# The first modulation blocks of a two-block transformer kernel with the weight tile as the moving operand of TensorE, and another order at the stage's end

## The chip, the cores and the metric

The kernel runs on one core of one Trainium2 chip. The metric is the device time in microseconds (us), the median of several executions; lower is better. Engines are named as in the profile: PE is TensorE's matmul, PEld its weight load, DVE VectorE, ACT ScalarE, POOL GpSimd, SP the engine that issues the DMAs. Sizes in MB are 10^6 bytes.

## The reference

Two transformer blocks on one sequence of 256 tokens, width 2048, in fp32. Only the head of the first block matters here:

```python
c_act = jax.nn.silu(c)                              # [1, 2048]
mod = c_act @ w_ada[l] + b_ada[l]                   # w_ada: [2048, 12288]
sh1, sc1, gt1, sh2, sc2, gt2 = jnp.split(mod, 6, axis=-1)
h = modulate(rmsnorm(x, g_norm_mix[l]), sh1, sc1)   # rmsnorm(x) * (1 + sc1) + sh1
proj = h @ w_in[l]                                  # w_in: [2048, 3072]
```

After it come a gated linear recurrence and a pooling mixer, an output projection, a gated feed-forward layer and a second block with attention and a state-space part. The vector times matrix product `c_act @ w_ada` reads 100 MB of weights for one row of result, and `w_in` cannot start before the first third of it (shift and scale) is there.

## The kernel before

The program is written by hand, one instruction stream for each engine, with semaphores between them. The columns of `w_ada` are cut into 12 blocks of 1024 columns, and each block into 16 row chunks of 128: a **slot** is one chunk of one block, 128x1024 fp32, 0.524 MB. The **first stage** works off blocks 0 to 3 (`MOD_FIRST`, shift and scale, in the order `MOD_ORDER`): 64 slots, through a ring of 8 buffers (`mod_raw` and `mod_more`). The other blocks are spread over later phases.

The order of everything is fixed in the code. SP issues the slots in order; the DMA of slot s waits until slot s-8 has been used (`load_first`, L477). In the same queue stand the small vectors (L544), x (L546) and the four 1.05 MB tiles of `w_in`'s first block (L498), at the places of the table `w_in_at`. A table `mod_on_pe` gives each slot to one of two engines: in blocks 0 and 1 the odd chunks are PE's, in blocks 2 and 3 the chunks 1, 4, 7, 10 and 13; that is 26 slots for PE and 38 for DVE.

- DVE's share (L1972, L1976): `mod_acc = slot * c_silu[:, k] + mod_acc`, an elementwise sum over chunks that leaves 128 partial sums in each column.
- PE's share (`first_product`, L1245): eight matmuls with a 128x128 piece of the slot as the stationary operand and the one column `c_silu[:, k:k+1]` moving. The result is one PSUM column for each 128 outputs.
- `first_sums` (L1253) at a block's end: eight more such matmuls add DVE's partial sums over the partitions onto the same PSUM columns. `first_result` (DVE, L1982) adds the bias and signals `mod_ready`.

PE's stream in the stage also holds the transposes of the small vectors (`turn_vectors`, L1224, behind chunk 11 of block 0, which wait until all the small loads have landed), four blocks of transposes of x (`turn_block`, L1161) and, behind chunk 15 of block 2 and chunks 5 and 11 of block 3, halves 0, 1 and 2 of `w_in`'s first block (`first_w_in`, L1108 to L1110). A **half** is two row chunks by 512 columns, 24 matmuls with 256 moving columns; it needs ACT's `w_hi` (L613) and DVE's `w_lo` (L1719), the split of the raw tile, and two chunks of the normed and modulated input, `a_hi` and `a_lo` (L700, L1815), which DVE scales in `scaled` (L1994). Halves 0 to 3 need blocks 0 and 1 of the modulation only, halves 4 to 7 need all four.

After the last sums SP may overwrite old buffers with `gates_w` and `pool_w` (it waits for a POOL memset, L461, that waits for `mod_mm`), and only then issues the next tiles of `w_in` (L498) and slots 66 and up (L486). Then the phase `w_in` runs: for each of its 48 halves ACT and DVE split, DVE works off 1.25 slots (`mod_beside`, L1950), and PE does 24 matmuls.

```python
for m in range(MOD_M):        # PE, one slot, before: L1244
    mm = pe.matmul(first_column(i, m), first_slot(s)[:, m * P:(m + 1) * P], c_silu[:, k:k + 1],
                   start=(k == 1 and m == 0), stop=False, skip_group_check=True)
```

## Time and profile before

| | |
|---|---|
| median of 3 runs | 2711.17 us (2710.86 to 2712.18) |
| the profiled execution | 2713.19 us, its span 2711.5 us |
| mean granted clock of TensorE | 0.982 of full speed |
| PE busy | 2637.1 us (97%) |
| PEld busy | 2250.8 us (83%) |
| DVE busy | 1655.9 us (61%) |
| ACT busy | 1246.0 us (46%) |
| the 16 DMA engines | 548.50 MB, mean 202 GB/s over the span |

The shares of the whole span say little of a stage of some 130 us at its start. So the views of that stretch count: the windows (busy time of each engine, granted clock and DMA rate by stretch), the chain of waits (what released what) and the timeline.

### The profile page before, as it was taken

To read this page: it belongs to the slowest core of one execution; us is meant where nothing else is said; L and a number is where in the kernel's file an instruction comes from. 1 tells how busy PE (TensorE), PEld (TensorE's weight loads), DVE (VectorE), ACT (ScalarE), POOL (GpSimd) and SP (SyncE) were. 2 spreads that over 40 slices of the span, in tenths; PEclk is the share of its full clock that TensorE was granted. 3 is DMA by queue.
4 is the path that set the end of the run, shared out by engine and by line. 5 is a ranking of instruction groups with operands and counts; after the bars stand their busy time and mean duration, and the time that the engine had idled before them with its cause. 6 is when DMAs were issued, how large, how long until landed. Compare 5 with 4: busy or idle time off the path is not lost.

```text
span 2711.5 us, 34305 instructions
## 1 busy us (share of the span) xinstructions
PE 2637.1 (97%) x13318; PEld 2250.8 (83%) x13318; DVE 1655.9 (61%) x1954; ACT 1246.0 (46%) x1591; POOL 5.6 (0%) x24
## 2 busy tenths in 40 slices
PE   8999989999999999989999999999999999999998
PEld 8989767888888888878899988888888888888877
DVE  3598887674545444454866677555666666644445
ACT  2146335444444434443566555444555555544453
POOL 0000000000000000000000000000000000000000
PEclk9899999999999999988999999999999999999999
DMA  8897897885555555544543443555555555555554
GB/s 310 307 380 267 314 356 243 282 272 186 186 186 189 183 188 182 181 151 135 176 140 110 156 140 123 173 188 192 185 184 184 185 184 185 186 194 187 182 202 140
DMA packets 350003, 548.50 MB, mean 202 GB/s; under 512 B 18481, under 2 KB 200769, under 8 KB 349249
## 3 DMA queue, kind: packets, MB, share of 16 engines
q1 hardware_dynamic: 349888, 546.90, 59.9%
q8 instruction: 82, 1.34, 0.2%
q14 instruction: 33, 0.26, 0.0%
HBM read 544.74 MB, written 2.10 MB: 202 GB/s over the span
## 4 chain that ended last, share of the span: by engine, by line
PE 85%; DVE 6%; DMA 4%; ACT 3%; issue 2%; SPq 1%; ACTq 0%; DVEq 0%
PE pair L1133 23%; PE pair L1135 23%; PE pair L1134 23%; DMA mod_raw<-in_w_ada 3%; PE pair L1245 2%; PE pair L1108 2%; PE pair L1109 2%; PE pair L1110 2%; DVE mod_acc L1950 2%; DVE w_lo L1719 1%; PE misc L1161 1%; PE pair L1646 1%; ACT w_hi L613 1%; PE misc L1581 1%; PE misc L1699 1%
## 5 line engine op out<-in xcount | busy, mean ns | idle before, releaser
L1719 DVE TENSOR_TENSOR w_lo<-raw,w_hi 128x1024 fp32r<-128x1024 f32 x848 | 1017.4, 1204 | 877.4 <-ACT w_hi L613 876.2
L613 ACT ACTIVATE w_hi<-raw 128x1024 fp32r<-128x1024 f32 x848 | 882.0, 1043 | 1120.1 <-PE pair L1135 1027.0
L1133 PE MATMUL pair<-w_hi,a_hi 128*128 128x512 f32 x1856 | 733.8, 395 | 9.0 <-DVE w_lo L1719 3.8
L1135 PE MATMUL pair<-w_hi,a_lo 128*128 128x512 f32 x1856 | 725.7, 391 | 0.0
L1134 PE MATMUL pair<-w_lo,a_hi 128*128 128x512 f32 x1856 | 725.2, 391 | 0.0
L1133 PEld LDWEIGHTS pair<-w_hi,a_hi 128*128 128x128 f32 x1856 | 350.4, 189 | 82.8 <-issue 6.7
L1135 PEld LDWEIGHTS pair<-w_hi,a_lo 128*128 128x128 f32 x1856 | 350.0, 189 | 74.0
L1134 PEld LDWEIGHTS pair<-w_lo,a_hi 128*128 128x128 f32 x1856 | 350.4, 189 | 71.9 <-issue 1.0
L1133 PE MATMUL pair<-w_hi,hid_hi 128*128 128x512 f32 x704 | 274.7, 390 | 0.0
L1135 PE MATMUL pair<-w_hi,hid_lo 128*128 128x512 f32 x704 | 274.0, 389 | 0.0
L1134 PE MATMUL pair<-w_lo,hid_hi 128*128 128x512 f32 x704 | 273.9, 389 | 0.0
L1108 PE MATMUL pair<-a_hi,w_hi 128*128 128x256 f32 x768 | 228.2, 297 | 14.4 <-issue 8.6
L1109 PE MATMUL pair<-a_lo,w_hi 128*128 128x256 f32 x768 | 221.8, 289 | 0.0
L1110 PE MATMUL pair<-a_hi,w_lo 128*128 128x256 f32 x768 | 221.6, 289 | 0.0
L1108 PEld LDWEIGHTS pair<-a_hi,w_hi 128*128 128x128 f32 x768 | 152.2, 198 | 19.4 <-issue 9.1
L1950 DVE SCALAR_TENSOR_TENSOR mod_acc<-mod_raw,keep,mod_acc 128x1024 f32<-128x1024 f32 x120 | 153.7, 1281 | 17.9 <-DMA mod_raw<-in_w_ada 15.2
L1135 PEld LDWEIGHTS pair<-w_hi,hid_lo 128*128 128x128 f32 x704 | 132.1, 188 | 27.6
L1133 PEld LDWEIGHTS pair<-w_hi,hid_hi 128*128 128x128 f32 x704 | 132.2, 188 | 27.3
L1134 PEld LDWEIGHTS pair<-w_lo,hid_hi 128*128 128x128 f32 x704 | 132.2, 188 | 27.0
L1109 PEld LDWEIGHTS pair<-a_lo,w_hi 128*128 128x128 f32 x768 | 152.2, 198 | 0.1
L1110 PEld LDWEIGHTS pair<-a_hi,w_lo 128*128 128x128 f32 x768 | 151.8, 198 | 0.0
L1133 PE MATMUL pair<-w_hi,ya_hi 128*128 128x512 f32 x128 | 50.6, 395 | 0.9 <-DVE w_lo L1719 0.9
(358 smaller groups left out, 2284.6 us busy)
## 6 DMA issues: line engine op xcount, KB each, us to landing
raw<-in_w_in SPq DMA_DIRECT2D x88, 1024.0 KB, 5.4
raw<-in_w_up SPq DMA_DIRECT2D x176, 512.0 KB, 4.3
mod_raw<-in_w_ada SPq DMA_DIRECT2D x160, 512.0 KB, 6.5
raw<-in_w_out SPq DMA_DIRECT2D x48, 1024.0 KB, 5.1
raw<-in_w_ffn_gate SPq DMA_DIRECT2D x88, 512.0 KB, 3.6
raw<-in_w_ffn_up SPq DMA_DIRECT2D x88, 512.0 KB, 4.6
raw<-in_w_ffn_down SPq DMA_DIRECT2D x32, 1024.0 KB, 5.1
raw<-in_w_down SPq DMA_DIRECT2D x32, 1024.0 KB, 5.0
```

What stands on the lines that cost most here:

```text
L613: run(w_hi[:, h % HALF_SLOTS, 0:n, :], raw[:, h // 2 % RAW_SLOTS, at0:at0 + n, :], ACT.Copy).then_inc(hi_ready, 1)
L1108: pe.matmul(o, wh, hi[:, k, :], start=(h == kk == 0 and m % 2 == 0), stop=False, skip_group_check=True)
L1109: pe.matmul(o, wh, lo[:, k, :], start=False, stop=False, skip_group_check=True)
L1110: mm = pe.matmul(o, wl, hi[:, k, :], start=False, stop=(h == ph.halves - 1 and kk == n - 1), skip_group_check=True)
L1133: pe.matmul(o, hi[:, own], w_hi[:, slot, kk, :], start=(h == kk == 0), stop=False)
L1134: pe.matmul(o, hi[:, own], w_lo[:, slot, kk, :], start=False, stop=False)
L1135: mm = pe.matmul(o, lo[:, own], w_hi[:, slot, kk, :], start=False, stop=(h == ph.halves - 1 and kk == n - 1))
L1161: mm = pe.transpose(misc[:, m % 4 // 2, m % 2 * S + t * P:m % 2 * S + (t + 1) * P], src[:, t, m * P:(m + 1) * P], ident[:])
L1245: mm = pe.matmul(first_column(i, m), first_slot(s)[:, m * P:(m + 1) * P], c_silu[:, k:k + 1], start=(k == 1 and m == 0), stop=False, skip_ ...
L1581: mm = pe.matmul(misc[:, h // 8, (h % 8) * SP:(h % 8 + 1) * SP], decay[:, h, :], xdt[:, c, h, :], start=True, stop=True, skip_group_check= ...
L1719: dve.tensor_tensor(w_lo[:, slot, 0:n, :], raw[:, h // 2 % RAW_SLOTS, at0:at0 + n, :], w_hi[:, slot, 0:n, :].bitcast(F32), ALU.subtract).t ...
L1950: dve.scalar_tensor_tensor(out=acc, in0=of, scalar=by, in1=acc, op0=ALU.mult, op1=ALU.add).then_inc(mod_step, 1)
```

## The change

PE's product takes the slot as the moving operand: two matmuls of 512 columns with `c_silu[:, k]` spread over 128 stationary columns. The result is a row of 1024 sums in PSUM (the same on each partition), in `pair` or, for block 2, in two banks of `misc`. A new DVE step `add_rows` adds this row to partition 0 of `mod_acc` once PE's last product of the block is done, and `first_sums` then makes the columns of the sum, as before with eight matmuls of one moving column. At the stage's end half 3 of `w_in` stands right behind the last sums in PE's stream, and the splits of halves 3, 4 and 5 stand before the end of the stage or among the scaling steps. `turn_vectors` moves from behind chunk 11 to behind chunk 13, and the third `w_in` tile from slot 58 to slot 61 of SP's queue.

```diff
@@ tables and counts
-    FIRST_BY_DVE, FIRST_BY_PE = mod_on_pe.count(False), mod_on_pe.count(True)
+    FIRST_BY_DVE = mod_on_pe.count(False) + MOD_FIRST
+    ROWS_AFTER = 14
...
+        def first_rows(i):
+            return (pair[:, 0], pair[:, 1], misc[:, 2:4], pair[:, 1])[i]
...
+        FIRST_SPLIT = 6
@@ SP
-            w_in_at = {2 * KC + 8: 0, 3 * KC: 1, 3 * KC + 10: 2, 3 * KC + 15: 3}
+            w_in_at = {2 * KC + 8: 0, 3 * KC: 1, 3 * KC + 13: 2, 3 * KC + 15: 3}
@@ ACT
                 norm_high(0, q)
-                if q < LEAD:
+                if q < XG // 2:
                     split_hi(w_in, 0, [q])
+                if q == XG // 2 - 1:
+                    split_hi(w_in, 0, [4])
+                elif q == XG - 2:
+                    split_hi(w_in, 0, [5])
@@ PE
             def first_product(i, k):
...
+                if i == 3 and not mods_of_pe(i, k):
+
+                    pe.wait_ge(mod_ready, 2)
+                for e in range(2):
+                    mm = pe.matmul(first_rows(i)[:, e, :], c_silu[:, k:k + 1].to_broadcast([P, P]), first_slot(s)[:, e * COLS:(e + 1) * COLS],
+                                   start=(mods_of_pe(i, k) == 0), stop=(mods_of_pe(i, k) + 1 == mods_of_pe(i)))
+                mm.then_inc(mod_used, 1)
+
+            def first_sums(i):
+
+                pe.wait_ge(mod_step, steps_of_dve(i + 1))
                 for m in range(MOD_M):
-                    mm = pe.matmul(first_column(i, m), first_slot(s)[:, m * P:(m + 1) * P], c_silu[:, k:k + 1],
-                                   start=(k == 1 and m == 0), stop=False, skip_group_check=True)
...
+                    mm = pe.matmul(first_rows(i)[:, 0, m:m + 1], mod_acc[:, i % 2, m * P:(m + 1) * P], ones[:, 0:1],
+                                   start=True, stop=True, skip_group_check=True)
                 mm.then_inc(mod_mm, 1)
...
-                    if (i, k) == (0, 11):
+                    if (i, k) == (0, 13):
                         turn_vectors()
...
                 first_sums(i)
-
-
-            pe.wait_ge(mod_ready, MOD_FIRST)
+            first_w_in(3)
...
-                features(w_in, b, b % 2, a_hi, a_lo, pools if b == 5 else None, normed_yet(0) if b == 0 else None, LEAD if b == 0 else 0)
+                features(w_in, b, b % 2, a_hi, a_lo, pools if b == 5 else None, normed_yet(0) if b == 0 else None, 4 if b == 0 else 0)
@@ DVE
+            def add_rows(i):
+
+                dve.wait_ge(mod_used, mod_on_pe[:(i + 1) * KC].count(True))
+                dve.wait_ge(mod_step, steps_of_dve(i + 1) - 1 - (KC - 1 - ROWS_AFTER if not mod_on_pe[i * KC + KC - 1] else 0))
+                acc = mod_acc[0:1, i % 2, :].rearrange("p (e n) -> p e n", e=2)
+                dve.tensor_tensor(acc, acc, first_rows(i)[0:1], ALU.add).then_inc(mod_step, 1)
...
-                elif (i, k) in ((3, 3), (3, 6)):
-                    split_lo(w_in, 0, [k // 3])
+                elif (i, k) in ((3, 3), (3, 6), (3, 11)):
+                    split_lo(w_in, 0, [{3: 1, 6: 2, 11: 3}[k]])
...
                     if not mod_on_pe[i * KC + k]:
                         first_product(i, k)
                         first_beside(i, k)
+                    if k == ROWS_AFTER:
+                        add_rows(i)
+            split_lo(w_in, 0, [4])
             first_result(MOD_FIRST - 1)
...
+                if q == XG - 2:
+                    split_lo(w_in, 0, [5])
...
-                    split_lo(ph, b1, [h % w_in.halves])
+                    if b or n >= FIRST_SPLIT - LEAD:
+                        split_lo(ph, b1, [h % w_in.halves])
```

**Two places in the order of the instructions.** The first is PE's stream at the end of block 0 (`mod_more_78` and the like are buffers of the ring; x8 counts matmuls). Before:

```order
L1245 MATMUL pair<-keep,mod_raw 128x1 x16
L1224 MATMUL misc<-ident,vec_rows 128x128 x7
L1245 MATMUL pair<-keep,mod_more_77 128x1 x8
L1245 MATMUL pair<-keep,mod_more_78 128x1 x8
L1253 MATMUL pair<-ones,mod_acc 128x1 x8
```

With the change:

```order
L1263 MATMUL pair<-mod_raw,keep 128x512 x4
L1263 MATMUL pair<-mod_more_77,keep 128x512 x2
L1242 MATMUL misc<-ident,vec_rows 128x128 x7
L1263 MATMUL pair<-mod_more_78,keep 128x512 x2
L1271 MATMUL pair<-ones,mod_acc 128x1 x8
```

Each slot of PE's is two matmuls of 512 columns in place of eight of one, the transposes of the vectors (L1224, now L1242) stand one slot later, and the eight matmuls of the sums are as many as before.

The second place is DVE's stream at the end of the stage, from the last products of block 3 on. Before (L1976 is a product, L1982 the result, L1719 a `w_lo` split, L1946 and L1950 products of block 4):

```order
L1976 SCALAR_TENSOR_TENSOR mod_acc<-mod_more_78,keep,mod_acc 128x1024 x2
L1982 TENSOR_TENSOR mod<-pair,vec 128x8
L1986 SCALAR_TENSOR_TENSOR keep<-mod,vec 128x8
L1994 TENSOR_SCALAR features_70<-features_70,keep,mod 128x256 x4
L1815 TENSOR_TENSOR a_lo<-features_70,a_hi 128x512
L1994 TENSOR_SCALAR features_70<-features_70,keep,mod 128x256 x2
L1815 TENSOR_TENSOR a_lo<-features_70,a_hi 128x512
L1994 TENSOR_SCALAR features_70<-features_70,keep,mod 128x256 x2
L1815 TENSOR_TENSOR a_lo<-features_70,a_hi 128x512 x2
L1719 TENSOR_TENSOR w_lo<-raw,w_hi 128x1024
L1946 TENSOR_SCALAR mod_acc<-mod_raw,keep 128x1024
```

With the change:

```order
L1994 SCALAR_TENSOR_TENSOR mod_acc<-mod_more_78,keep,mod_acc 128x1024
L2007 TENSOR_TENSOR mod_acc<-mod_acc,pair 1x1024
L1994 SCALAR_TENSOR_TENSOR mod_acc<-mod_more_78,keep,mod_acc 128x1024
L1737 TENSOR_TENSOR w_lo<-raw,w_hi 128x1024
L2000 TENSOR_TENSOR mod<-pair,vec 128x8
L2011 SCALAR_TENSOR_TENSOR keep<-mod,vec 128x8
L2019 TENSOR_SCALAR features_70<-features_70,keep,mod 128x256 x4
L1833 TENSOR_TENSOR a_lo<-features_70,a_hi 128x512
L2019 TENSOR_SCALAR features_70<-features_70,keep,mod 128x256 x2
L1833 TENSOR_TENSOR a_lo<-features_70,a_hi 128x512
L1737 TENSOR_TENSOR w_lo<-raw,w_hi 128x1024
```

The new L2007 (`add_rows`) stands between the last two products, the split of half 4 stands before the result, and that of half 5 before the last scaling; behind them come four products of block 4 in a row before the split of half 6.

## Rows read from the trace of the kernel before

**Rows 1.** Windows: stretch and length, then busy us PE, PEld, DVE, ACT, POOL; PEclk, DMA share, GB/s.

```profile
0.00:42.00 42.00, 29.31 (x136) 29.04 (x136) 13.37 (x21) 7.83 (x10) 3.77 (x23) 1.00 0.88 332
50.00:100.00 50.00, 50.00 (x237) 50.00 (x238) 24.34 (x48) 11.91 (x16) 0.00 (x0) 1.00 0.86 287
100.00:120.00 20.00, 20.00 (x123) 20.00 (x122) 13.77 (x15) 1.58 (x2) 0.00 (x0) 0.74 1.03 408
130.00:138.00 8.00, 0.24 (x3) 0.16 (x2) 7.25 (x15) 4.00 (x6) 1.81 (x1) 0.53 0.43 108
138.00:165.00 27.00, 25.03 (x185) 24.65 (x186) 21.57 (x19) 11.56 (x14) 0.00 (x0) 0.89 1.04 396
165.00:212.00 47.00, 44.33 (x347) 42.53 (x347) 46.69 (x58) 18.94 (x22) 0.00 (x0) 1.00 1.00 370
```

**Rows 2.** Chain of waits that ended last, to 170 us: start, us, what.

```profile
23.13 10.61 DMA rows<-in_k_norm_g
...
42.21 3.41 PE pair L1253 x16
...
62.69 1.81 PE misc L1161 x8
...
128.46 1.80 PE pair L1253 x16
130.28 0.18 DVE mod L1982
```

**Rows 3.** Groups of instructions of the first 150 us, shapes apart.

```profile
L1245 PE MATMUL pair<-keep,mod_more 128*128 128x1 f32 x224 | 45.9, 336 | 2.5 <-DMA mod_more<-in_w_ada 2.5
L1245 PE MATMUL pair<-keep,mod_raw 128*128 128x1 f32 x192 | 40.1, 341 | 4.1 <-DMA mod_raw<-in_w_ada 4.1
...
L1976 DVE SCALAR_TENSOR_TENSOR mod_acc<-mod_more,keep,mod_acc 128x1024 f32<-128x1024 f32 x18 | 23.1, 1282 | 19.7 <-DMA mod_more<-in_w_ada 19.3
...
L1719 DVE TENSOR_TENSOR w_lo<-raw,w_hi 128x1024 fp32r<-128x1024 f32 x7 | 8.5, 1219 | 0.3 <-ACT w_hi L613 0.3
```

**Rows 4.** Timeline of the stage, PE: start us, us, engine, line, operation.

```profile
45.49 6.96 PE L1245 MATMUL pair<-keep,mod_raw 128*128 128x1 f32 x32
...
102.59 0.41 PE L1109 MATMUL pair<-a_lo,w_hi 128*128 128x256 f32 x1
...
102.81 0.41 PE L1110 MATMUL pair<-a_hi,w_lo 128*128 128x256 f32 x1
...
103.21 0.28 PE L1109 MATMUL pair<-a_lo,w_hi 128*128 128x256 f32 x1
...
105.87 2.91 PE L1245 MATMUL pair<-keep,mod_raw 128*128 128x1 f32 x16
...
117.11 1.84 PE L1245 MATMUL pair<-keep,mod_more 128*128 128x1 f32 x16
```

**Rows 5.** Timeline, PE: fp32 matmuls of 512 moving columns elsewhere in the kernel.

```profile
2614.78 7.03 PE L1699 MATMUL misc<-w_ple,p_f 128*128 128x512 f32 x16
```

**Rows 6.** Timeline, PE: a short idle time and matmuls of 64 columns.

```profile
1420.67 0.28 PE L1110 MATMUL pair<-a_hi,w_lo 128*128 128x256 f32 x1
1422.17 0.41 PE L1435 MATMUL misc<-v_t,p_tr 128*128 128x64 f32 x2 [1.22 <-DVE scores L2283]
...
1425.15 0.41 PE L1109 MATMUL pair<-a_lo,w_hi 128*128 128x256 f32 x1
```

**Rows 7.** The line L2146: duration ns min/median/max, first and last start.

```profile
L2146 DVE TENSOR_TENSOR res_tmp<-pair,row x8: 1215/1218/1225, 336.5 to 1175.5; 128x1024 f32<-128x1024 f32 x8
```

**Rows 8.** Timeline of the stage's end, DVE and SP's queue.

```profile
123.37 2.67 DVE L1976 SCALAR_TENSOR_TENSOR mod_acc<-mod_more,keep,mod_acc 128x1024 f32<-128x1024 f32 x2 [1.16 <-DMA mod_more<-in_w_ada]
...
136.23 1.28 SPq L486 DMA_DIRECT2D mod_raw<-in_w_ada  x2
...
137.50 1.23 DVE L1719 TENSOR_TENSOR w_lo<-raw,w_hi 128x1024 fp32r<-128x1024 f32 x1 [0.25 <-ACT w_hi L613]
...
145.45 1.29 DVE L1950 SCALAR_TENSOR_TENSOR mod_acc<-mod_raw,keep,mod_acc 128x1024 f32<-128x1024 f32 x1 [3.53 <-DMA mod_raw<-in_w_ada]
```

More of the change, by code:

```diff
@@ L151, in two_blocks, with mods_of_pe, steps_of_dve @@
     mod_on_pe = [k in ((1, 3, 5, 7, 9, 11, 13, 15), (1, 4, 7, 10, 13))[i // 2] for i in range(MOD_FIRST) for k in range(KC)]
-    FIRST_BY_DVE, FIRST_BY_PE = mod_on_pe.count(False), mod_on_pe.count(True)
+    FIRST_BY_DVE = mod_on_pe.count(False) + MOD_FIRST
+    ROWS_AFTER = 14
     def mods_used(s):
-        return mod_on_pe[:s + 1].count(mod_on_pe[s])
+        own = mod_on_pe[:s + 1].count(mod_on_pe[s])
+        return own if mod_on_pe[s] else own + (s // KC + (s % KC > ROWS_AFTER))
+    def mods_of_pe(i, k=KC):
+        return mod_on_pe[i * KC:i * KC + k].count(True)
+    def steps_of_dve(i):
+        return mod_on_pe[:i * KC].count(False) + i
     def mod_at(place):
@@ L791, in mixer @@
                     ph, b1 = (w_in, b) if h < w_in.halves else (w_in, b + 1) if b + 1 < w_in.blocks else (w_out, 0)
-                    split_hi(ph, b1, [h % w_in.halves])
+                    if b or n >= FIRST_SPLIT - LEAD:
+                        split_hi(ph, b1, [h % w_in.halves])
                     beside(b, n)
@@ L1243, in first_product @@
                 pe.wait_ge(mod_landed[s % FIRST_SLOTS], 16 * (s // FIRST_SLOTS + 1))
-                for m in range(MOD_M):
-                    mm = pe.matmul(first_column(i, m), first_slot(s)[:, m * P:(m + 1) * P], c_silu[:, k:k + 1],
-                                   start=(k == 1 and m == 0), stop=False, skip_group_check=True)
+                if i == 3 and not mods_of_pe(i, k):
[3 more added lines that the diff above has]
+                                   start=(mods_of_pe(i, k) == 0), stop=(mods_of_pe(i, k) + 1 == mods_of_pe(i)))
                 mm.then_inc(mod_used, 1)
             def first_sums(i):
-                pe.wait_ge(mod_step, (i + 1) * KC - mod_on_pe[:(i + 1) * KC].count(True))
+                pe.wait_ge(mod_step, steps_of_dve(i + 1))
                 for m in range(MOD_M):
-                    mm = pe.matmul(first_column(i, m), mod_acc[:, i % 2, m * P:(m + 1) * P], ones[:, 0:1],
-                                   start=False, stop=True, skip_group_check=True)
+                    mm = pe.matmul(first_rows(i)[:, 0, m:m + 1], mod_acc[:, i % 2, m * P:(m + 1) * P], ones[:, 0:1],
+                                   start=True, stop=True, skip_group_check=True)
                 mm.then_inc(mod_mm, 1)
@@ L1292, in _ @@
             for b in range(w_in.blocks):
-                if 2 <= b < 4:
+                if b == 1:
+                    pe.wait_ge(mod_ready, MOD_FIRST)
+                elif 2 <= b < 4:
                     pe.wait_ge(c1_tap, 12 * (b - 1))
@@ L1981, in first_result @@
                 dve.wait_ge(mod_mm, i + 1)
-                dve.tensor_tensor(mod[:, own], pair[:, i // 2, i % 2, 0:MOD_M], b_ada[:, own], ALU.add).then_inc(mod_ready, 1)
+                dve.tensor_tensor(mod[:, own], first_rows(i)[:, 0, 0:MOD_M], b_ada[:, own], ALU.add).then_inc(mod_ready, 1)
+            def add_rows(i):
[3 more added lines that the diff above has]
+                dve.tensor_tensor(acc, acc, first_rows(i)[0:1], ALU.add).then_inc(mod_step, 1)
             def modulated_gain(scale, g, own=slice(0, KC)):
```

3 lines of the change are left out of this document (1 added, 2 removed).

## The prediction

> **What bounds the kernel now.** I read the windows first, then the chain of waits, then the timeline, all for the first 170 us; the change touches nothing behind them. The windows [rows 1] show PE busy for all of 50 to 100 us, while DVE is busy for 24.34 of these 50 us and the DMA engines move 287 GB/s; from 100 to 120 us they move 408 GB/s, so they can do more. The chain [rows 2] agrees: the last of the small loads lands at 33.74, then it runs through PE's L1245, L1161 and L1253 to the result of block 3 at 130.28. **The first stage is PE's.** PE spends 45.9 + 40.1 = 86 us in its 26 products [rows 3], and two products take 6.96 us [rows 4], so one takes some 3.41 us of PE's queue (16 instructions; each fp32 matmul is issued twice).
>
> From 138 to 165 us the DMA is full (396 GB/s), and from 165 to 212 DVE is (46.69 of 47 us) [rows 1]. A stage that ends earlier moves that whole train earlier as long as the bytes come earlier too; so I count bytes.
>
> **What sets PE's price is its clock.** The row of granted clock says 1.00 to 100 us [rows 1], but the durations there are those of the lower level, 1.2 GHz: 256-column matmuls take 0.41 us until 102.81 and 0.28 us from 103.21 on [rows 4], after a run of such matmuls without a break. A product of 16 one-column instructions costs 3.41 us at the lower level and 1.84 at the higher [rows 4]. Such products do not keep the higher level, though PE never idles between them: the 16 that start at 105.87, behind sums of the same kind, again take 2.91 us.
>
> **The change, part by part.**
>
> *The products.* 8 fp32 matmuls, 512 columns each, take 7.03 us for 16 instructions at the higher level [rows 5]; without the last one's tail of 0.59 that is (7.03 - 0.59) / 15 = 0.43 us each. A product is now 2 matmuls, 4 instructions: 1.72 us, and at half the clock 3.43. **At the lower clock the change gives nothing; at the higher it halves 26 products, 44 us less work.** No row shows fp32 matmuls of 512 columns raising the clock; it was up when the one group began. I take it that they do, as PE streams columns in them without a break, which it also does in the 256-column matmuls that raised it.
>
> *Does PE then keep up?* After block 0's products, at 42.2 us [rows 2], PE has at the lower clock: 18 products (61.4), four sums of 3.41 (13.6), four turns of x at 1.81 (7.2) [rows 2], three halves of w_in at 24 matmuls 0.21 us apart (15.3) [rows 4]: 97.6 us; at the higher about 50. PE is fast enough for the end that I find below (69 us later) if not over a third to two fifths of its work runs at the lower level.
>
> *What ends the stage then: bytes.* To the landing of slot 63 SP must bring 64 x 0.524 (slots) + 2.10 (x) + 3 x 1.05 (tiles) + about 0.55 (small vectors) = 39.35 MB. At 42 us 0.332 x 42 = 13.94 MB were moved [rows 1]. I leave this part as it is: PE's first products wait for landings and the transposes for 33.74. From 42 to 48 us little is gained, since no slot of PE's is freed until the sums of block 0 (3.41 us) and a first product are through: two slots, 15.0 MB at 48 us. The remaining 24.35 MB at 0.400 (between 0.396 and 0.408) take 60.9 us: slot 63 lands at 108.9. DVE needs less: block 3 is 11 products, a norm step, three splits and the new step, some 19 us, beside 10.5 MB, 26 us.
>
> *The new step.* `add_rows` reads PSUM, 1024 elements a partition. Between nothing and 2.3 us (twice the nearest); the nearest row, an fp32 add of 1024 columns out of PSUM, is 1.22 us [rows 7], and I take it. Three of the four lie beside other work. In the last block it stands between DVE's last two products: 1.22 + 1.28 = 2.5 us from the landing to the sums, at 111.4. While it waits for PE's last product, DVE's next product and the slot it frees are queued behind it; in blocks 0 and 1 PE also waits 1.3 us for it before the sums. With 8 buffers that is hidden if PE is not behind; bound 0 to 3 x 1.3 = 3.9 us, I take nothing for it apart from the two slots above.
>
> *The last sums.* PE has been idle or in one-column work, so 3.41 us and not the 1.80 that they took here [rows 2]: the end is at 114.8 in place of 130.26. **15.5 us.** The waits that vanish there (PE's own queue) are replaced by DVE's and PE's on landings.
>
> *The order at the end.* Before, PE was idle behind the sums (busy 0.24 us from 130 to 138 [rows 1]), since the split of half 3 stood behind all the scaling (137.50 [rows 8]). Now half 3 covers the scaling, and three splits (3.7 us of DVE) have left the path behind the sums. But the chain there goes through DMA: slots 66 and 67 are issued 6 us after the sums (136.23) and the first is used at 145.45, after a wait of 3.53 us [rows 8], and SP's queue waits there as before. So the gain lies between 0 and 3.7; I take 2.5. SP's third tile issued three slots later changes no sum of bytes: nothing. `turn_vectors` one slot later: nothing, PE waited for 33.74 anyway.
>
> **Sum:** 15.5 + 2.5 = 18.0 us. Against the profiled execution, 2713.19 - 18.0 = 2695.2 us; that execution is 2.0 us above the median of the runs, so the forecast of the median is **2693 us**.
>
> **The rivals.** A measurement of this kernel can tell 0.2%, 5.4 us, from no change.
>
> 1. *Bytes, as above*: 12 to 24 us less, 2687 to 2699. Chance 0.55.
> 2. *The DMA is full from 44 us on at 0.417*, and the sums are fast: 24.9 MB / 0.417 = 60 us, end at 108, tail 3.7: 26 us less, 2685. Rows 1 show 408 for 20 us only. 0.07.
> 3. *The DMA does not hold 0.400.* From 165 to 212 us it moved 0.370 at a share of 1.00 [rows 1]: 65.8 us in place of 60.9, 13 us less, 2698. The Trainium skill speaks for it (HBM Reference, Specifications and the text below them): about 358 GB/s for a core whose neighbour streams too, about 425 for one alone; by 358 the bytes would take 68 us and the time would be 2700. Rows 1 have 408, so the neighbour seems to be quiet. 0.08.
> 4. *The clock does not hold.* At 1.72 us of work for two slots' arrival (1.05 MB / 0.400 = 2.6 us) PE now has gaps; in the attention part 1.2 us of idle time and a few 64-column matmuls were followed by a lower clock, 0.41 us for 256 columns again [rows 6]. Against it: once PE falls behind, its columns are dense again. With two thirds of the list at the lower level it takes 97.6 x 0.83 = 81 us, end 123.6, 9 us less, 2702. 0.14.
> 5. *The change does not do what it says*: the clock never rises for these products. They cost 3.43 for 3.41, PE waits 1.3 us for `add_rows` in two blocks and 2.5 in the last (+5.1), the tail gives back 2.5 or more: 2711 to 2714. 0.10.
> 6. *Slower*: as 5, and the tail loses. Four products of block 4 now stand before the split of half 6 in DVE's queue; slots 66 and 67 land late, PE runs dry after half 5 and does half 6 at the lower level, 24 x (0.213 - 0.115) = 2.4 us more: 5.1 + 2.4 = +7.5, 2718.7. It decides if a product of L1263 stays over 3.2 us. 0.06.
>
> The page TensorE: Matmul & The Clock Gate (HAM oscillation) of the Trainium skill holds idle gaps responsible for a fall of the clock. By it alone the stage before, with no gap in PE from 50 to 100 us, would have run at full clock, its products 1.87 us each; the rows have 3.41, so here the kind of work counts, not only the gaps, and that is why I give case 1 more than case 4.
>
> **How the numbers follow.** The forecast is case 1's middle. The range takes in cases 1 to 4 with some play, 2685 to 2706, and leaves out 5 and 6. Faster by over 0.2%: 0.55 + 0.07 + 0.08 + 0.14 = 0.84; within 0.2%: 0.09; slower: 0.07 (case 6 and a little of 5).
>
> **What would show it.** In the profile after: a group L1263 of 104 instructions 0.43 us apart for most of the stage (over 0.8 apart: case 5); windows from 50 to 105 us near 400 GB/s (case 1), with idle PE; DVE's wait ends on landings of `w_ada`, not on PE; L2007 at 1.2 us, four times; the last result near 115 us (before 130.28); half 3 right behind the last sums; slot 73's product some 18 us earlier than before, and the same distance kept to the end of the kernel. If the last result comes early and the end does not move, the phase behind it had a bound of its own, and the forecast is wrong by that.

## The result, and the profile after

| | before | after |
|---|---|---|
| median of the runs | 2711.02 us (2710.59 to 2712.18, 4 runs) | 2694.39 us (2693.5 to 2695.1, 4 runs) |
| ratio, with its 95% interval | | 0.9938 (0.9921 to 0.9955) |
| profiled execution, span | 2713.19 us, 2711.5 us | 2694.49 us, 2692.8 us |

The change makes the kernel 16.6 us faster (0.6%). The forecast was 2693 us, with a range of 2685 to 2706, so the measured time lies inside it. The two spans differ by 18.7 us, because the profiled execution of before was 2 us above its median and that of after was not.

The windows of the changed kernel, with the columns of [rows 1]:

```profile
0.00:42.00 42.00, 24.82 (x54) 11.26 (x55) 12.56 (x17) 7.83 (x10) 3.76 (x23) 0.88 0.91 340
50.00:100.00 50.00, 40.98 (x164) 24.28 (x162) 40.18 (x64) 12.85 (x18) 0.00 (x0) 0.90 1.02 400
100.00:120.00 20.00, 14.71 (x77) 13.16 (x76) 13.16 (x18) 3.89 (x5) 1.80 (x1) 0.74 0.67 241
130.00:138.00 8.00, 3.66 (x17) 3.67 (x18) 5.96 (x5) 1.19 (x2) 0.00 (x0) 0.50 1.04 399
```

From 50 to 100 us the DMA engines now move 400 GB/s where they moved 287, PE has 9 us of idle time where it had none, and DVE is busy for 40.2 of 50 us where it was for 24.3. But from 100 to 120 us only 241 GB/s are left of 408: the experiments with the gates (the block weights `gates_w` of the recurrence, below) are about that hole.

The groups of instructions of the first 135 us, shapes apart:

```profile
L1263 PE MATMUL pair<-mod_more,keep 128*128 128x512 f32 x44 | 24.7, 692 | 8.5 <-DMA mod_more<-in_w_ada 8.5
L1263 PE MATMUL pair<-mod_raw,keep 128*128 128x512 f32 x40 | 23.6, 730 | 5.6 <-DMA mod_raw<-in_w_ada 5.6
...
L1263 PE MATMUL misc<-mod_more,keep 128*128 128x512 f32 x12 | 5.7, 602 | 1.9 <-DMA mod_more<-in_w_ada 1.9
L1263 PE MATMUL misc<-mod_raw,keep 128*128 128x512 f32 x8 | 5.7, 857 | 2.4 <-DMA mod_raw<-in_w_ada 2.4
```

These 104 instructions are busy for 24.7 + 23.6 + 5.7 + 5.7 = 59.7 us, against 86 us for the 416 of [rows 3]. The idle time before them, which ends on landings of `w_ada` as it did before, is now 18.4 us in place of 6.6. The busy time is not 26 x 1.72 = 44.7 us, in the main because the clock does not stay up: six of the 26 products run at the lower level. The timeline of PE shows products at both levels (start us, us, and in brackets the wait before):

```profile
20.46 3.58 PE L1263 MATMUL pair<-mod_more,keep 128*128 128x512 f32 x4 [3.20 <-DMA mod_more<-in_w_ada]
23.87 1.88 PE L1263 MATMUL pair<-mod_raw,keep 128*128 128x512 f32 x4
26.48 1.98 PE L1263 MATMUL pair<-mod_raw,keep 128*128 128x512 f32 x4 [0.73 <-DMA mod_raw<-in_w_ada]
32.05 3.78 PE L1263 MATMUL pair<-mod_more,keep 128*128 128x512 f32 x4 [3.59 <-DMA mod_more<-in_w_ada]
...
60.60 3.02 PE L1271 MATMUL pair<-ones,mod_acc 128*128 128x1 f32 x16 [1.66 <-DVE mod_acc L2007]
63.47 3.76 PE L1263 MATMUL misc<-mod_raw,keep 128*128 128x512 f32 x4
...
75.31 1.98 PE L1263 MATMUL misc<-mod_raw,keep 128*128 128x512 f32 x4 [2.42 <-DMA mod_raw<-in_w_ada]
```

Behind waits of 3.20 and 3.59 us a product takes 3.58 and 3.78 us, the durations of the 1.2 GHz level; behind 0.73 us it takes 1.98, behind 2.42 us also 1.98, and without a wait 1.88, those of 2.4 GHz. Long waits are not the only thing that a fall follows: the products at 63.47 and 88.26 have no wait before them, stand right behind the one-column sums of a block (these behind waits of 1.66 and 1.80 us), and take 3.76 and 3.48 us.

The end of the stage, timeline of DVE and PE:

```profile
106.36 1.28 DVE L1994 SCALAR_TENSOR_TENSOR mod_acc<-mod_more,keep,mod_acc 128x1024 f32<-128x1024 f32 x1 [2.94 <-DMA mod_more<-in_w_ada]
107.75 1.21 DVE L2007 TENSOR_TENSOR mod_acc<-mod_acc,pair 1x1024 f32<-1x1024 f32 x1
109.06 1.28 DVE L1994 SCALAR_TENSOR_TENSOR mod_acc<-mod_more,keep,mod_acc 128x1024 f32<-128x1024 f32 x1
...
110.39 3.57 PE L1271 MATMUL pair<-ones,mod_acc 128*128 128x1 f32 x16 [5.29 <-DVE mod_acc L1994]
...
114.00 0.17 DVE L2000 TENSOR_TENSOR mod<-pair,vec 128x8 f32<-128x8 f32 x1 [2.52 <-PE pair L1271]
```

The last result of the stage comes at 114.00 us in place of 130.28 [rows 2]: 16.3 us earlier. This is the chain that the prediction wrote down: a landing (of slot 62), a product, `add_rows`, the last product, sums at the lower clock.

Behind it, timelines of DVE and of SP's queue (compare [rows 8]):

```profile
99.10 1.75 SPq L499 DMA_DIRECT2D mod_raw<-in_w_ada  x2
115.86 1.40 SPq L568 DMA_DIRECT2D gates_w<-in_w_rg_a  x2
...
118.66 0.62 SPq L570 DMA_DIRECT2D pool_w<-in_w_pool  x1
119.32 0.58 SPq L511 DMA_DIRECT2D raw<-in_w_in  x1
119.95 1.85 SPq L499 DMA_DIRECT2D mod_raw<-in_w_ada  x2
```

```profile
130.47 2.67 DVE L1968 SCALAR_TENSOR_TENSOR mod_acc<-mod_raw,keep,mod_acc 128x1024 f32<-128x1024 f32 x2 [5.18 <-DMA mod_raw<-in_w_ada]
133.06 1.22 DVE L1737 TENSOR_TENSOR w_lo<-raw,w_hi 128x1024 fp32r<-128x1024 f32 x1
...
147.57 1.28 DVE L1968 SCALAR_TENSOR_TENSOR mod_acc<-mod_raw,keep,mod_acc 128x1024 f32<-128x1024 f32 x1 [0.50 <-DMA mod_raw<-in_w_ada]
```

SP issues nothing from 100.9 to 115.9 us. Its queue stands in front of the gates' loads, whose tile is cleared only behind the last sums. Slots 66 and 67 are issued at 119.95 behind the gates, `pool_w` and a tile; DVE waits 5.18 us for them, and the split of half 6 (133.06) is queued behind that wait. PE waits 9.25 us for this split. The product of slot 73, at 162.77 before, runs at 147.57: of 16.3 us, 15.2 are left.

Followed further by the starts of some operations (all from timelines; `res_tmp` is written at the end of each of the four blocks of w_out, the output projection behind w_in, and `diag_a` in the phase behind w_out):

| us | last result | first `res_tmp` (w_out, block 0) | last `res_tmp` (block 3) | `diag_a` | output's first DMA issue |
|---|---|---|---|---|---|
| before | 130.28 | 336.54 | 419.89 | 425.56 | 2674.64 |
| after | 114.00 | 322.11 | 401.21 | 406.88 | 2655.94 |
| earlier by | 16.28 | 14.43 | 18.68 | 18.68 | 18.70 |

So in this pair of traces the stage brings 16.3 us, w_in gives back 1.9, and w_out, which the change does not touch, brings 4.2. From there to the end of the kernel nothing is lost or won.

### The profile page after: what moved, and what is told of

Same layout as the page of the kernel before. It is cut to its first block, busy times and chain, and to the rows that moved or that the text cites. A ratio compares the mean times of both kernels' runs of the same rounds, so it can differ in the third digit from the quotient of the medians.

```text
span 2692.8 us, 33691 instructions
## 1 busy us (share of the span) xinstructions
PE 2603.6 (97%) x13006; PEld 2181.9 (81%) x13006; DVE 1660.3 (62%) x1958; ACT 1245.9 (46%) x1591; POOL 5.6 (0%) x24
## 4 chain that ended last, share of the span: by engine, by line
PE 83%; DVE 7%; DMA 4%; ACT 3%; issue 2%; SPq 1%; ACTq 0%; DVEq 0%
PE pair L1151 23%; PE pair L1153 23%; PE pair L1152 23%; DMA mod_raw<-in_w_ada 3%; PE pair L1126 2%; PE pair L1127 2%; PE pair L1128 2%; DVE mod_acc L1968 2%; DMA mod_more<-in_w_ada 1%; DVE w_lo L1737 1%; PE pair L1664 1%; ACT w_hi L626 1%; DVE mod_acc L1994 1%; PE misc L1599 1%; PE misc L1717 1%
## 5 line engine op out<-in xcount | busy, mean ns | idle before, releaser
L1968 DVE SCALAR_TENSOR_TENSOR mod_acc<-mod_raw,keep,mod_acc 128x1024 f32<-128x1024 f32 x120 | 153.8, 1282 | 16.4 <-DMA mod_raw<-in_w_ada 13.6
```

Source lines behind the costliest of these rows:

```text
L1968: dve.scalar_tensor_tensor(out=acc, in0=of, scalar=by, in1=acc, op0=ALU.mult, op1=ALU.add).then_inc(mod_step, 1)
```

## The experiments

All times below are medians, and each ratio is to runs of the kernel before on the same chip in the same session (medians 2710.93, 2711.83 and 2712.41 us in the three sessions), with its 95% interval. Points of time inside the kernel are read from one trace of each kernel, and such traces scatter: in four kernels with the new products and nearly the same first stage (after, products_only, gates_later, gates_free) the last result comes at 114.00, 114.60, 114.64 and 115.79 us. A difference under some 2 us between two traces is not safe.

### Each half of the change alone: order_only and products_only

order_only is the kernel before with the new order at the stage's end; of its edits:

```diff
                 first_sums(i)
-
-
-            pe.wait_ge(mod_ready, MOD_FIRST)
+            first_w_in(3)
...
+            split_lo(w_in, 0, [4])
             first_result(MOD_FIRST - 1)
...
-                    split_lo(ph, b1, [h % w_in.halves])
+                    if b or n >= FIRST_SPLIT - LEAD:
+                        split_lo(ph, b1, [h % w_in.halves])
```

products_only is the changed kernel with exactly these edits undone.

> The kernel before, with its products as they were, and only the new order at the stage's end (third tile issued three slots later, half 3 of w_in right behind the last sums, splits of halves 3 to 5 moved, four products of block 4 ahead of the split of half 6). Theory of the prediction: the last result stays within 0.5 us of 130.28, and the path behind it gets 0 to 3.7 us shorter, 2.5 taken: 2707.3 to 2711.0, 2708.5 the likeliest. Rival, from the trace of the changed kernel (result 16.3 us earlier, but the product of slot 73 only 15.2 us earlier): the new order gives back about 1 us, since DVE waits for the bytes of slots 66 and 67 ahead of the split of half 6: 2711.5 to 2713.

> The changed kernel with its new products, but the old order at the stage's end. Theory of the prediction (products 15.5 us, order 2.5 us): last result within 0.7 us of 114.0, time 2694.4 + 2.5 = 2696.9. Rival (the order gives back 1 us): 2693.3. If the two parts depend on each other (the new order pays only where PE waits for landings), order_only and products_only do not add up to the whole -16.6 us.

| | median us | ratio | last result | first `res_tmp` |
|---|---|---|---|---|
| order_only | 2713.25 (11 runs) | 1.0008 (0.9999 to 1.0017) | 130.57 | 338.25 |
| products_only | 2693.09 (5 runs) | 0.9938 (0.9925 to 0.9952) | 114.60 | 321.59 |

The whole gain is the products'. The new order, expected at 2.5 us, brings nothing: in one pair it is 2.3 us on the wrong side, just inside the interval, which leaves room for a gain of 0.3 us at most; in the other the ratio is the same with it and without it (0.9938), with intervals too wide to tell 2.5 us. In the traces it costs 207.68 - 206.26 = 1.4 us from the last result to the first `res_tmp` in one pair, 208.11 - 206.99 = 1.1 us in the other; that it costs anything is within the scatter. The first line is PE's timeline of products_only, the second that of the changed kernel:

```profile
123.14 0.55 PE L1120 MATMUL pair<-a_hi,w_hi 128*128 128x256 f32 x1 [8.58 <-issue]
```

```profile
134.34 0.58 PE L1126 MATMUL pair<-a_hi,w_hi 128*128 128x256 f32 x1 [9.25 <-DVE w_lo L1737]
```

DVE's timeline of products_only:

```profile
121.82 1.23 DVE L1731 TENSOR_TENSOR w_lo<-raw,w_hi 128x1024 fp32r<-128x1024 f32 x1 [0.25 <-ACT w_hi L625]
...
129.15 1.28 DVE L1962 SCALAR_TENSOR_TENSOR mod_acc<-mod_raw,keep,mod_acc 128x1024 f32<-128x1024 f32 x1 [2.92 <-DMA mod_raw<-in_w_ada]
```

The old order has PE wait 8.58 us ahead of half 3, whose split (121.82) stands behind all the scaling; the new one has it wait 9.25 us ahead of half 6. The wait was moved, not removed. In both orders DVE then waits for slots 66 and 67: 2.92 us in the old one and 5.18 us in the new one, and there the split of half 6 is queued behind it.

### Does the stage end by its bytes? fewer_bytes, short_products, fewer_short

```diff
-                sp.dma_start(first_slot(s), ada[:, s % KC, bass.ds(MOD_ORDER[s // KC] * MOD_COLS, MOD_COLS)]).then_inc(mod_landed[s % FIRST_SLOTS], 16)
+                cols = MOD_COLS if s < FIRST_SLOTS else MOD_COLS - P
+                sp.dma_start(first_slot(s)[:, 0:cols], ada[:, s % KC, bass.ds(MOD_ORDER[s // KC] * MOD_COLS, cols)]).then_inc(mod_landed[s % FIRST_SLOTS], 16)
```

> The changed kernel, but from the ninth slot on each load of w_ada in the first stage brings 896 of the 1024 columns, so 56 x 65.5 KB = 3.67 MB less (the last 128 columns of these slots are computed from what the buffer held before; every engine does the same work). Theory (the stage ends by its bytes at 0.400 GB/us): the last result comes 9.2 us earlier, at 105 to 107 in place of 114.0, and the time falls by about as much, to 2685 to 2687. Rival (PE's clock or DVE's 80 per cent of busy time carry the stage as well): less than 4 us, last result behind 110.

```diff
-                    mm = pe.matmul(first_rows(i)[:, e, :], c_silu[:, k:k + 1].to_broadcast([P, P]), first_slot(s)[:, e * COLS:(e + 1) * COLS],
+                    n = COLS if not mods_of_pe(i, k) else P
+                    mm = pe.matmul(first_rows(i)[:, e, 0:n], c_silu[:, k:k + 1].to_broadcast([P, P]), first_slot(s)[:, e * COLS:e * COLS + n],
```

> The changed kernel, but all of PE's products in the first stage except the first one of each block take 128 columns in place of each 512 (the other columns of PE's part are left out of the result). PE then has 22 products of a quarter of the columns. Theory (bytes bound the stage, PE's price no longer matters, at either clock): last result within 1 us of 114.0 and time within 1.5 us of 2694.4. Rival (the 3.4 to 3.8 us that products took at the lower clock delay the slots' release and so the loads): last result 3 us or more earlier, 2688 to 2691. A third outcome: with PE idle most of the time the clock is low for half 3 of w_in, up to 2 us slower.

Both edits together:

> The changed kernel with both of the earlier edits: 56 loads of w_ada bring 896 of 1024 columns, and PE's products, but for the first of each block, take 128 columns in place of each 512 (so the last columns and most of PE's part are left out of the result). fewer_bytes alone moved the last result from 114.0 only to 112.03, and its DMA share from 42 to 100 us fell to 0.93, 344 GB/s; short_products alone left it at 114.37. Theory A (once the bytes are fewer, PE's products at the lower clock are the next bound): last result at 108 to 110. Theory B (DVE, busy 46 of 58 us with waits between, or the order in which slots are freed by it, is the next bound): last result stays within 1 us of 112.0.

| | median us | ratio | last result |
|---|---|---|---|
| fewer_bytes | 2689.81 (4 runs) | 0.9911 (0.9896 to 0.9927) | 112.03 |
| short_products | 2694.66 (4 runs) | 0.9939 (0.9924 to 0.9955) | 114.37 |
| fewer_short | 2689.61 (4 runs) | 0.9914 (0.9899 to 0.9929) | 109.24 |

The windows from 42 to 100 us, first of fewer_bytes, then of fewer_short:

```profile
42.00:100.00 58.00, 51.80 (x184) 29.76 (x184) 46.01 (x72) 17.29 (x20) 0.00 (x0) 0.86 0.93 344
```

```profile
42.00:100.00 58.00, 40.85 (x209) 33.18 (x208) 47.27 (x72) 17.29 (x20) 0.00 (x0) 0.79 0.97 371
```

Quartering PE's products alone leaves the last result where it was (+0.4 us), as a stage bound by bytes should. But 3.67 MB less bring 2.0 us at the last result, not 9.2: there the rival won that run. (The time fell by more, 4.6 us between the medians, and the first `res_tmp` by 4.4 us; where the rest comes from is not shown.) A part of the 9.2 was never there, since loads of 896 columns move fewer bytes in the same busy time (344 / 0.93 = 370 GB/s for a full share in fewer_bytes and 371 / 0.97 = 382 in fewer_short, against 400 / 1.02 = 392 for 1024 columns). By these rates the 56 loads would save 5.5 to 7.6 us (25.7 MB at 382 to 370 for 29.4 MB at 392), an estimate. The DMA share falls to 0.93, so loads now wait for free slots, and with short products too the result comes another 2.8 us earlier: theory A. **The bytes are the bound, but PE's products stand close behind them, some 2 us as far as single traces tell.** With both edits 4.8 us were had, near what the bytes could give by the estimate; whether DVE, busy for 47 of 58 us, takes part too is not shown. The prediction's picture of PE as fast enough holds; its picture of a stage with room is too good.

### What the new step costs: rows_twice

```diff
+                dve.tensor_tensor(res_tmp[0:1], acc, first_rows(i)[0:1], ALU.add)
                 dve.tensor_tensor(acc, acc, first_rows(i)[0:1], ALU.add).then_inc(mod_step, 1)
```

> The changed kernel with a second DVE addition of PE's rows in each of the four add_rows (into a scratch tile, so the result is unchanged): 4 x 1.21 us of DVE. Prediction's reading: three of the four lie beside other work and the last is on the path to the sums, so the last result is 1.2 us later, 115.2, and the time 0 to 1.2 us longer. Rival (a step in which DVE holds up its next product, the slot it frees and PE's sums costs in every block): last result 3 to 5 us later, 117 to 119, time 2697 to 2699.

Measured: 2700.42 us (4 runs), ratio 0.9951 (0.9936 to 0.9966), 6.0 us above the changed kernel by the medians, and 3.5 us by the ratios, whose intervals touch; last result at 122.84, which is 8.8 us later and far outside the scatter. That is more than the four additions themselves (4.8 us). Block 0, timelines of DVE and PE:

```profile
40.97 1.21 DVE L2007 TENSOR_TENSOR res_tmp<-mod_acc,pair 1x1024 f32<-1x1024 f32 x1 [3.59 <-PE pair L1263]
42.11 1.20 DVE L2008 TENSOR_TENSOR mod_acc<-mod_acc,pair 1x1024 f32<-1x1024 f32 x1
```

```profile
37.32 3.62 PE L1263 MATMUL pair<-mod_more,keep 128*128 128x512 f32 x4 [1.44 <-DMA mod_more<-in_w_ada]
43.37 2.98 PE L1271 MATMUL pair<-ones,mod_acc 128*128 128x1 f32 x16 [2.43 <-DVE mod_acc L2008]
46.21 5.99 PE L1263 MATMUL pair<-mod_raw,keep 128*128 128x512 f32 x8
```

In the changed kernel PE's last product of block 0 starts at 37.12 and takes 2.00 us, the first addition starts at 39.16, the sums at 40.42 take 1.95 us, and the two products behind them 3.68 us. Here the sums start 2.95 us later. But 1.81 us of that was there before anything differs between the two kernels: the last product took 3.62 us at the lower level, and the first addition starts at 40.97. The step itself adds the other 1.14 us (PE waits 2.43 us for DVE in place of 1.30). The sums then take 2.98 us and the two products 5.99 us; as the level was down already ahead of the added step, this trace cannot say that the step brought that on. By the last block DVE's addition is 7.7 us late (115.44 for 107.75), and the DMA share from 42 to 100 us is 0.92. With the 1.8 us taken off, some 7 us remain at the last result for 1.2 us more in each block, where the prediction's reading has 1.2 us in all. So the rival is right in kind and even too small: the step is not hidden in the first blocks. How the 7 us divide between the step, PE's clock and chance is not shown, and they are not the price of the single step.

### The hole behind the stage: gates_later, gates_later_b4

```diff
-            sp.wait_ge(zeroed, 2)
-            for n, w in enumerate((d["w_rg_a"][0], d["w_rg_i"][0])):
...
             for b in range(1, w_in.blocks):
                 load_beside(w_in, b, plain(d["w_in"][0], bass.ds(w_in_cols[b], COLS)))
+                if b == 1:
+                    sp.wait_ge(zeroed, 2)
+                    for n, w in enumerate((d["w_rg_a"][0], d["w_rg_i"][0])):
...
```

> The changed kernel with the loads of the gates and of pool_w moved in SP's queue from behind slot 65 to behind block 1 of w_in. In the changed kernel SP's queue stands from 100.9 to 115.9 us for the memset of the gates (itself behind the last sums), and the DMA engines move 85 GB/s from 110 to 120. Theory (the bytes bound the phases behind the stage too): tiles 4 and 5 and slots 66 and 67, 3.1 MB or 7.9 us at 400 GB/s, land in that gap; DVE's wait of 5.18 us at 130.47 goes, the time falls by 4 to 8 us to 2686 to 2690. Rival (behind 165 us DVE is the bound and DVE has the same work to do): no more than the 5.18 us and likely less, since DVE next waits for tiles whose buffers come free late: 2692 to 2694.4.

> The same move of the loads of the gates and pool_w, in the kernel before. There SP's queue stands from 120.8 to 132.1. Theory of bytes: 2711.0 less 4 to 7 us. Rival: DVE's and PE's work behind the last sums bounds that part, within 1.5 us of 2711.0. If both kernels gain alike, the gap is independent of the change.

Measured: gates_later 2694.68 us (5 runs), ratio 0.9942 (0.9928 to 0.9956); gates_later_b4 2713.06 us (11 runs), ratio 1.0006 (0.9997 to 1.0015). Nothing in either kernel, much as the rivals said (gates_later_b4 is 2.1 us above its before by the medians, where its rival had 1.5 at most), but for another reason than theirs. DVE's wait of 5.18 us is gone and slot 73's product runs at 142.31, 5.3 us earlier. Then, DVE's timeline of gates_later:

```profile
145.43 2.67 DVE L1969 SCALAR_TENSOR_TENSOR mod_acc<-mod_raw,keep,mod_acc 128x1024 f32<-128x1024 f32 x2
...
155.78 1.28 DVE L1969 SCALAR_TENSOR_TENSOR mod_acc<-mod_raw,keep,mod_acc 128x1024 f32<-128x1024 f32 x1 [5.76 <-DMA mod_raw<-in_w_ada]
```

The gates and `pool_w` are 1.6 MB. SP now issues them from 138.44 to 145.00 us, ahead of the next slots, in a stretch where the DMA is full, and DVE then waits 5.76 us for a slot, where the changed kernel has no wait of DVE for slots at all between 149 and 170 us: what was won is given back.

### The same hole, filled: gates_free, free_early, free_before

The gates' tile lies where the rows of the vectors lay. These are last read by PE ahead of the sums of block 0, so the memset need not wait for block 3:

```diff
-            pool.wait_ge(mod_mm, MOD_FIRST)
+            pool.wait_ge(mod_mm, 1)
             pool.memset(gates_w[:], 0.0).then_inc(zeroed, 1)
```

That is gates_free; free_before is the same line in the kernel before; free_early adds:

```diff
             split_lo(w_in, 0, [4])
+            mod_beside(0)
             first_result(MOD_FIRST - 1)
...
-                    mod_beside(b * w_in.halves + n)
+                    if b or n:
+                        mod_beside(b * w_in.halves + n)
```

> The changed kernel; the memset of the gates' tile waits for the sums of block 0 in place of those of block 3, and nothing else is altered. SP's queue then does not stand from 100.9 to 115.9 us, and the gates, pool_w, tiles 4 and 5 and slots 66 and 67 (4.7 MB, 11.7 us at 400 GB/s) are moved in that gap; unlike in gates_later, the gates' bytes do not come back in front of slots at 145 us, where they cost DVE a wait of 5.76 us. Theory (the gain of gates_later ahead of 145 us, 5.3 us at slot 73, is kept): 2687 to 2691. Rival (behind 165 us DVE, then PE, are the bound and their work is the same; the stretch up to there has its own waits): 2693 to 2695.

> As gates_free, and DVE does the products of slots 64 and 65 ahead of the last result of the stage (while it waits 2.5 us for PE's sums) in place of behind the scaling. Takes 2.0 us out of DVE's queue ahead of the split of half 6, and frees slots 64 and 65 some 10 us earlier, so SP need not stand from 107 to 124 us for slot 68. Theory: 1 to 3 us less than gates_free. Rival: slots 64 and 65 land too late (issued at 99 to 101 us behind tiles of 1 MB), DVE waits for them ahead of the stage's last result, and the time is 0 to 2 us longer than that of gates_free.

> The kernel before, with the memset of the gates' tile waiting for the sums of block 0 only. There SP's queue stands from 120.8 to 132.1 us. Theory: the same gap as in the changed kernel, 3 to 6 us less than 2711.0. Rival (the gap is worth nothing without the new products, as DVE has then no train to catch up with): within 1 us. It also tells whether the stretch of w_out, first to last res_tmp, 83.35, 81.64 and 81.66 us in three kernels with the old products and 79.1 to 79.9 us in seven with the new, goes by the products: 81 to 84 us here if it does, about 79 if it goes by how early the stage's loads are through.

| | median us | ratio | last result | first `res_tmp` | first to last `res_tmp` |
|---|---|---|---|---|---|
| gates_free | 2688.56 (5 runs) | 0.9918 (0.9905 to 0.9932) | 115.79 | 317.02 | 79.32 |
| free_early | 2688.74 (5 runs) | 0.9920 (0.9906 to 0.9934) | 115.88 | 314.56 | 79.24 |
| free_before | 2706.25 (11 runs) | 0.9982 (0.9973 to 0.9991) | 129.68 | 330.46 | 82.37 |

Two windows of gates_free, then the second of them in gates_later, then SP's queue of gates_free:

```profile
100.00:120.00 20.00, 14.38 (x68) 12.12 (x69) 12.46 (x18) 3.32 (x5) 0.00 (x0) 0.78 1.06 341
118.00:126.00 8.00, 8.00 (x55) 8.00 (x55) 6.69 (x11) 5.30 (x7) 0.00 (x0) 0.77 1.06 389
```

```profile
118.00:126.00 8.00, 7.03 (x58) 6.73 (x56) 6.70 (x11) 5.30 (x8) 0.00 (x0) 1.00 0.36 113
```

```profile
102.76 4.91 SPq L568 DMA_DIRECT2D gates_w<-in_w_rg_a  x2
...
116.48 1.11 SPq L499 DMA_DIRECT2D mod_raw<-in_w_ada  x2
```

From 100 to 120 us the DMA moves 341 GB/s for 241 in the changed kernel, at a full share (the gates' small rows move less in the same time), and from 118 to 126 us there is no second hole, as gates_later has one with 113 GB/s. With the gates' bytes in the hole, the stretch from the last result to the first `res_tmp` shrinks from 208.11 to 201.23 us in the changed kernel and from 206.26 to 200.78 in the one before; by the ratios the time falls by 5.4 us (0.9938 to 0.9918) and by 4.9 us (1 to 0.9982). gates_free is the fastest by its median, 22 us below the kernel before; its interval and that of the change still touch, so against the changed kernel it is the trace (first `res_tmp` 5.1 us earlier, `diag_a` 402.01 for 406.88) that shows the gain. free_early is another 2.5 us earlier in its trace (`diag_a` at 399.47) and not in its median; whether it adds anything stays open. In both traces the last result is 1.8 to 1.9 us later than in the changed kernel's; dense_free, below, has the same memset and not this delay, so it goes for scatter.

### The clock under the last sums: dense_free

gates_free, with work for PE in its last wait:

```diff
             def first_sums(i):
...
+                if i == 3:
+                    pe.wait_ge(mod_ready, 3)
+                    for e in (0, 1, 0, 1, 0, 1):
+                        pe.matmul(misc[:, 2 + e, :], c_silu[:, 13:14].to_broadcast([P, P]), first_slot(61)[:, e * COLS:(e + 1) * COLS],
+                                  start=True, stop=True, skip_group_check=True)
                 pe.wait_ge(mod_step, steps_of_dve(i + 1))
```

> As gates_free, and PE repeats its last product of block 3 three times into a bank that nobody reads, in the 5.30 us in which it waits for DVE ahead of the last sums (12 instructions of 512 columns, 5.2 us at the higher clock level). Tests the term of the last sums (3.41 us at the lower level in the prediction, 3.58 measured in gates_free). Theory: dense columns keep the higher level, sums and half 3 run at it, the sums take 1.9 us, the last result comes 1.7 us earlier, 114.1 in place of 115.79, and the time is 1 to 2 us below that of gates_free (2688.6). Rival: the one-column sums bring the level down by themselves, or the repeats run over the wait; last result at 115.5 to 117, time 2688 to 2690.

PE's timeline, of dense_free and then of gates_free:

```profile
104.76 5.31 PE L1272 MATMUL misc<-mod_more,keep 128*128 128x512 f32 x12
110.27 1.95 PE L1276 MATMUL pair<-ones,mod_acc 128*128 128x1 f32 x16 [0.20 <-DVE mod_acc L1999]
```

```profile
112.18 3.58 PE L1271 MATMUL pair<-ones,mod_acc 128*128 128x1 f32 x16 [5.30 <-DVE mod_acc L1994]
```

The sums take 1.95 us in place of 3.58, as expected: what brought them to the lower level was the wait, and dense columns in it kept the level up. The last result is at 112.25, 3.5 us earlier; 1.6 of it is the sums, and 1.9 lie in a landing ahead of them (the last one that DVE waits for came at 106.23 in place of 108.14), which is scatter. But the time is 2690.3 us (5 runs), ratio 0.9917 (0.9904 to 0.9931): no gain over gates_free. In its trace DVE waits 1.71 us for slots 66 and 67 at 124.09, where gates_free had no such wait, and the first `res_tmp` is at 317.09 for 317.02. Of the 3.5 us, 1.6 are left at slot 73 (141.18 for 142.80) and none at the first `res_tmp`: the sums' clock is worth nothing there, in all likelihood because the train behind the stage is set by landings.

## Why the prediction was right

Time, sign and mechanism were right; the sum contains one term that did not come at all and leaves out one that nobody wrote down.

- **The products, and their price at both levels.** 104 instructions, 1.88 us a product with its tail at the higher level and 3.6 to 3.8 at the lower, against 1.72 (without tail) and 3.43: right. That columns of 512 raise the clock was an assumption without a row; 59.7 us for 26 products is 2.3 us each, nearer to the higher level than to the lower. The first two products of the kernel (6.66 us) ran at the lower level, and the next one, at 15.27, at the higher.
- **What ends the stage.** The byte count put slot 63 at 108.9 and the last result at 114.8; the last landing that DVE waits for, that of slot 62, comes at 106.36, slot 63 has landed some time before DVE reads it at 109.06, and the result is at 114.00. **15.5 us forecast, 16.3 measured.** The rate of 0.400 held (400 GB/s from 50 to 100 us). The sum of bytes has two errors that point the same way: from 42 to 48 us the DMA moved 351 GB/s and not two slots' worth, and the stretch to 42 us moved 340 and not 332 GB/s. So 16.4 MB and not 15.0 were through at 48 us, 3.5 us ahead of the forecast, and by the windows the 39.35 MB were through at about 105.6. The result is only 0.8 us early: slot 62 landed later than these bytes. SP issues the fourth tile and slots 64 and 65 from 98.62 on, and bytes of theirs may be among those counted; the sum left them out, and no run shows how many. The good figure owes something to that. short_products shows that PE does not bound it; fewer_bytes and fewer_short show that the next bound is close, some 2 us away, which the prediction did not say.
- **Rival 3 (the DMA does not hold 0.400)** is out: the DMA moved 400 GB/s for 50 us. The Trainium skill (HBM Reference, Specifications and the text below them) gives about 358 GB/s for a core whose neighbour streams too and about 425 for one alone. The 400 measured here lie between the two and above the first, so the first is not the case of these runs; what the neighbour did, no run shows.
- **Rival 4 (the clock does not hold)** happened in part: six of the 26 products run at the lower level (two from 7.44 us on, and those at 20.46, 32.05, 63.47 and 88.26), too few of them to matter. (Its end, 42.2 + 81, is 123.2 us and not 123.6, which changes nothing.) The Trainium skill (TensorE: Matmul & The Clock Gate, HAM oscillation) puts a fall of the clock down to PE's idle time in waits for DMA. In part the traces agree: waits of 3.20 and 3.59 us for DMA, and of 5.30 us for DVE, are followed by the lower level, and filling the last one kept the level up. The kernel before, with no waits and one-column matmuls at the lower level, is what that section alone does not explain, and neither are the products at 63.47 and 88.26, with no wait in front of them and one-column sums behind waits of only 1.66 and 1.80 us ahead of that.
- **`add_rows`.** The price, 1.22 us, is exact (1.20 to 1.21 us measured), though the row it came from is an addition over 128 partitions and this one has one. "Three of the four lie beside other work" failed: rows_twice is 8.8 us later at the last result, some 7 us when the difference ahead of the added step is taken off, and not 1.2. In the changed kernel PE waits 1.30, 1.66 and 1.80 us for DVE ahead of the sums of the first three blocks, where the prediction had 1.3 us in two of them. The single step's own cost in the first blocks was not measured alone; whether it lies within the bound of 3.9 us given for it is open.
- **The last sums.** 3.41 us at the lower clock forecast, 3.57 measured.
- **The order at the end: the step that failed.** 2.5 us forecast, bounds 0 to 3.7; measured at most 0.3 us by order_only's interval, and -1.1 and -1.4 us in the two pairs of traces, which is within their scatter. The three splits did leave the path behind the sums, but the four products that were put ahead of the split of half 6 wait there for slots 66 and 67. It is the second half of rival 6, which saw PE run dry behind half 5 but priced only the lower clock of half 6, 2.4 us, and not the wait, which is 9.25 us (before, PE waited 8.58 us ahead of half 3). "The chain there goes through DMA", written in the prediction as the reason to take less than the whole, should have been the sum.
- **"The same distance kept to the end"** held only from w_out's end on. Inside w_out, untouched by the change, 4.2 us were won in the profiled pair. From the first to the last `res_tmp` the four kernels with the old products take 81.64 to 83.35 us, the ten with the new ones 78.93 to 80.45, and free_before, which was run for this among others, falls among the old (82.37). Without the trace of before itself the old ones have a mean of 81.9 us, the new ones one of 79.6: some 2.3 us go with the products, and the rest of the 4.2 belongs to that one trace, whose execution was also 2 us above its median. That these 2.3 us, which nobody foresaw, made up for the 2.5 us of the order that did not come, is luck: without them the forecast would have been further off.

How these go together: 16.3 (stage) - 1.2 (order) - 0.6 (the rest of what w_in gave back) + 2.3 (w_out) is 16.8 us, beside 16.6 measured in the medians. Each term is read from one trace or a few, which scatter by 1 to 2 us, so that they agree to 0.2 us is chance.

What stays open is why w_out's stretch is shorter. In both kernels it is a closed loop there: SP's queue waits for DVE's products and splits, and DVE waits for landings. In before DVE's waits for `w_ada` sum to 8.7 us from 280 to 425 us, in after to 5.0 us from 266 to 406 us, the same work. Why the landings come later behind the old products is not shown by any run.

## What to carry to other kernels

When one engine stops being the bound, follow the queue that feeds the next phase as well: SP's queue stood for 15 us behind one memset whose wait was for far more than it needed, and one changed number there gave some 5 us, in the old kernel (clear of noise) as in the new (by its traces). Moving those loads later, where the DMA is full, gave nothing; bytes have to go where the DMA is idle, not only out of the way. And a term in which work is put ahead of a waiting split is to be priced by what that work waits for, not by the work that left the path.

## What the runs showed of the hardware that was not expected

- TensorE's level changes from one product to the next: 3.58 us behind a wait of 3.20 us, 1.88 us for the next one, 3.78 us behind 3.59 us; but behind 2.42 us of waiting a product still took 1.98 us. Sixteen one-column matmuls soon behind dense ones still ran at the higher level (1.95 us), in dense_free and at 40.42 and 86.45 us in the changed kernel; behind a wait of 5.3 us they took 3.57 us. The dense product right behind those of 86.45 us, with no wait, took 3.48 us.
- Loads of 128 x 896 fp32 moved 370 GB/s (fewer_bytes) and 382 GB/s (fewer_short) for a full share of the DMA engines, those of 128 x 1024 392.
- DVE's addition of one partition, 1 x 1024 out of PSUM, takes 1.21 us, the 128 x 1024 one 1.22 us [rows 7]: here the partitions cost nothing.
